# First attention's heads: column denominators, rows turned on TensorE, other step order

## What is computed

```python
w = jnp.exp(dmat - m_t[..., None]) * jnp.einsum('bhtd,bhsd->bhts', qc, kc)
num = jnp.einsum('bhts,bhsv->bhtv', w, vc) + wi[..., None] * jnp.einsum('bhvd,bhtd->bhtv', cm, qc)
den = jnp.sum(w, axis=-1) + wi * jnp.einsum('bhd,bhtd->bht', nv, qc)
h = num / jnp.maximum(jnp.abs(den), jnp.exp(-m_t))[..., None]
...
y = mlstm_readout(hl_f + rq(hl_b), ol, head_gain, w_out)   # norm of each head, gain, sigmoid(o), @ w_out
```

## Time and profile before

| | us |
|---|---|
| median of 3 runs | 1459.04 (1457.6 to 1459.34) |
| the profiled execution | 1456.49 |
| its span, first to last instruction | 1454.7 |
| PE busy | 1382.9 (95%) |
| DVE busy | 1146.6 (79%) |
| ACT busy | 784.0 (54%) |
| mean granted TensorE clock | 0.986 of 2.4 GHz |

### The profile page before, as it was taken

How to read it: one execution, slowest core, us unless ns; L and a number is a source line. 1 busy time by engine, 2 the same in 40 slices (tenths; PEclk the granted TensorE clock), 3 DMA queues, 4 the chain that set the end, 5 groups by cost and what they waited for, 6 DMA issues and landing times.

```text
span 1454.7 us, 19174 instructions
## 1 busy us (share of the span) xinstructions
PE 1382.9 (95%) x7530; PEld 1183.9 (81%) x7530; DVE 1146.6 (79%) x1629; ACT 784.0 (54%) x1114; POOL 1.4 (0%) x6
## 2 busy tenths in 40 slices
PE   6999988899998999999999999999999999999998
PEld 4888966788886888879887888878888888788886
DVE  5786688799977988878777988779889777887653
ACT  6613443666635555456356655376554555665542
POOL 0000000000000000000000000000000000000000
PEclk9999999999999999999999999999999999999999
DMA  9566413566793988866635877958878741585551
GB/s 384 214 244 249 147 49 130 219 254 234 258 340 138 327 289 293 319 233 229 251 129 187 306 277 287 335 192 302 286 287 304 269 154 60 202 280 198 187 189 58
DMA packets 62715, 337.79 MB, mean 232 GB/s; under 512 B 6929, under 2 KB 9361, under 8 KB 34209
## 3 DMA queue, kind: packets, MB, share of 16 engines
q1 hardware_dynamic: 62160, 335.35, 63.4%
q0 software_dynamic: 288, 1.05, 0.2%
q10 hardware_dynamic: 176, 0.16, 0.0%
HBM read 335.49 MB, written 1.05 MB: 231 GB/s over the span
## 4 chain that ended last, share of the span: by engine, by line
PE 80%; DVE 10%; ACT 5%; DMA 3%; issue 2%; SPq 0%; DVEq 0%; ACTq 0%
PE bank L253 77%; DVE wlo L249 2%; DMA raw<-w_stream 2%; ACT rstd L543 1%; ACT whi L242 1%; DVE mring L755 1%; ACT T L597 1%; DVE rd L1420 1%; PE bank L514 1%; DVE T L607 1%; DMA mring<-m_stream 1%; DVE SGC L672 1%; DVE X L685 1%; DVE EF L1422 0%; PE bank L730 0%
## 5 line engine op out<-in xcount | busy, mean ns | idle before, releaser
L253 PE MATMUL bank<-hh,whi 128*128 128x512 f32 (+1 forms) x2192 | 675.0, 368 | 8.3 <-DVE wlo L249 8.1
L249 DVE TENSOR_TENSOR wlo<-raw,whi 128x2048 fp32r<-128x2048 f32 x219 | 500.6, 2288 | 71.1 <-ACT whi L242 71.0
L253 PE MATMUL bank<-hh,wlo 128*128 128x256 f32 x1896 | 533.1, 281 | 0.0
L242 ACT ACTIVATE whi<-raw 128x2048 fp32r<-128x2048 f32 x219 | 418.4, 1915 | 163.6 <-PE bank L253 109.9
L253 PEld LDWEIGHTS bank<-hh,whi 128*128 128x128 f32 x2192 | 395.5, 190 | 85.0 <-DVE wlo L249 8.0
L253 PEld LDWEIGHTS bank<-hh,wlo 128*128 128x128 f32 x1896 | 360.5, 190 | 0.0
L253 PE MATMUL bank<-whi,hid_hi 128*128 128x512 f32 x440 | 172.2, 391 | 0.0
L253 PE MATMUL bank<-whi,hid_lo 128*128 128x512 f32 x440 | 171.3, 389 | 0.0
L253 PE MATMUL bank<-wlo,hid_hi 128*128 128x512 f32 x440 | 171.2, 389 | 0.0
L253 PE MATMUL bank<-whi,hh 128*128 128x512 f32 x480 | 158.4, 400 | 1.6 <-DVE hh L622 0.8
L755 DVE SCALAR_TENSOR_TENSOR mring<-mring,con 128x1024 f32<-128x1024 f32 x107 | 130.6, 1220 | 18.8 <-DMA mring<-m_stream 18.7
(11 more groups left out here) (293 smaller groups left out, 1305.2 us busy)
## 6 DMA issues: line engine op xcount, KB each, us to landing
raw<-w_stream SPq DMA_DIRECT2D x219, 1024.0 KB, 5.0
mring<-m_stream SPq DMA_DIRECT2D x139, 512.0 KB, 5.0
cb<-m_stream SPq DMA_DIRECT2D x53, 512.0 KB, 5.1
con<-const_d SPq DMA_DIRECT2D x1, 1472.0 KB, 11.4
XF<-xT SPq DMA_DIRECT2D x1, 1024.0 KB, 12.8
XC<-ctxT SPq DMA_DIRECT2D x1, 1024.0 KB, 12.8
y<-OUT SPq DMA_DIRECT2D x4, 256.0 KB, 2.6
cb<-c_row POOLq DMA_DIRECT2D x1, 512.0 KB, 7.7
```

The lines of the kernel that those rows point to most:

```text
L242: nc.scalar.activation(w_hi(c, 0, CW), raw[:, c % RAW_SLOTS], ACT.Copy).then_inc(s_hi, 1)
L249: nc.vector.tensor_tensor(w_lo(c, 0, CW), raw[:, c % RAW_SLOTS], w_hi(c, 0, CW).bitcast(f32), ALU.subtract).then_inc(s_lo, 1)
L253: return nc.tensor.matmul(out, lhsT, rhs, start=start, stop=True, skip_group_check=True)
```

## The change

Denominators are made as columns: `EF` is now the stationary operand and two columns of ones the moving one, so that the sums for 128 target tokens stand in 128 partitions of bank 3. ACT takes the absolute value of 128x4 numbers into `den`; DVE compares them with thresholds that were transposed once with `uc` (now 128x216), and inverts 128x4 numbers (`invert`). PE turns these columns into rows by four transposes of a broadcast column (`inverse_rows`) into the head's own bank, and `normalise` multiplies `EF` with that bank. `rows(h)` no longer broadcasts thresholds, `thb` is gone, the output gate moves to bank 5.

```diff
-        UP_UNITS = [[2, 1, 1, 0, 1] + [1, 0, 1, 1, 0] * 3 + [1, 0], [2, 1] + [1] * 20, [2, 1] + [1] * 20,
+        UP_UNITS = [[3, 2, 2, 1, 1] + [1, 0, 1, 1, 0] * 3 + [1, 0], [2, 1] + [1] * 20, [2, 1] + [1] * 20,
...
-                    mm(bank[2 + d][:, 0:SEQ], cst("sel")[0:36, q:q + P], mt[:], True)
-                    ins = mm(bank[2 + d][:, SEQ:], cst("sel")[0:36, q:q + P], th[:], True)
+                    ins = mm(bank[2][:, d * SEQ:(d + 1) * SEQ], cst("sel")[0:36, q:q + P], mt[:], True)
...
-                    for st in range(4):
-                        ins = mm(bank[5][:, d * SEQ:(d + 1) * SEQ], ones, EF[h % 2][:, d, st], st == 0)
+                    for t in range(2):
+                        at = 4 * t + 2 * d
+                        for st in range(4):
+                            ins = mm(bank[3][:, at:at + 2], EF[h % 2][:, d, st, t * P:(t + 1) * P], ones[:, 0:2],
+                                     st == 0)
                 ins.then_inc(s_den, 1)
 
-            def numerators(h):
-
-                pe.wait_ge(s_gw2, h + 1)
+            def inverse_rows(h):
+                pe.wait_ge(s_rc, h + 1)
                 if h >= 2:
                     pe.wait_ge(s_y, 2 * h - 2)
+                for d in range(2):
+                    for t in range(2):
+                        ins = nc.tensor.transpose(head_bank(h)[:, d * SEQ + t * P:d * SEQ + (t + 1) * P],
+                                                  den[:, h, t, d:d + 1].to_broadcast([P, P]), ident)
+                ins.then_inc(s_rb, 1)
...
+            for t in range(2):
+                ins = nc.tensor.transpose(bank[1][:, (4 + t) * 36:(5 + t) * 36], th[:, t * P:(t + 1) * P],
                                           ident[0:36, 0:36])
...
             denominators(0)
             scores(1)
+            inverse_rows(0)
+            rows(2)
             output_gate(2)
+            numerators(0)
             denominators(1)
             scores(2)
+            pe_stat(pe, N_LSTM)
+            inverse_rows(1)
             output_gate(3)
+            numerators(1)
+            rows(3)
+            denominators(2)
+            scores(3)
+            pe_stat(pe, N_LSTM + 1)
+            inverse_rows(2)
+            numerators(2)
+            denominators(3)
+            pe_stat(pe, N_LSTM + 2)
+            inverse_rows(3)
+            out_chunk(0)
+            numerators(3)
             pe.wait_ge(s_os, 4)
-            for h in range(HEADS):
-                if 1 <= h < HEADS - 1:
-                    denominators(h + 1)
-                if h == 1:
-                    scores(3)
-                if h >= 2:
-                    out_chunk(h - 2)
-                if h + 2 < HEADS:
-                    rows(h + 2)
-                numerators(h)
-                pe_stat(pe, N_LSTM + h)
-            pe.wait_ge(s_ad, HEADS)
             pe.wait_ge(s_y, 2 * HEADS - 2)
             pe_gate_row(pe, "lstm", (5, 6))
+            pe_stat(pe, N_LSTM + 3)
+            out_chunk(1)
             pe_out_last(pe, c + 15, 4, hhi, hlo, HEAD_TAIL, lambda: out_chunk(2), lambda: out_chunk(3))
...
+            def squares(h, table=False):
+                act_squares(act, N_LSTM + h, lambda j: head_bank(h)[:, j * SEQ:(j + 1) * SEQ],
+                            lambda j: (s_num, h + 1), table)
+
+            squares(0)
             magnitudes(1)
+            decay(2, 1)
+            decay(2, 0)
+            act_rstd(act, N_LSTM, DV)
             gate_read(3)
             act.wait_ge(s_os, 4)
             nc.scalar.activation(OS[:], OS[:], ACT.Sigmoid).then_inc(s_sg, 1)
-            for h in range(HEADS):
-                if 1 <= h < HEADS - 1:
-                    magnitudes(h + 1)
-                if h:
-                    round_head(h - 1)
-                    act_split(act, c + 14 + h)
-                if h + 2 < HEADS:
-                    decay(h + 2, 1)
-                act_squares(act, N_LSTM + h, lambda j: head_bank(h)[:, j * SEQ:(j + 1) * SEQ],
-                            lambda j: (s_num, h + 1), h == 0)
-                if h + 2 < HEADS:
-                    decay(h + 2, 0)
-                act_rstd(act, N_LSTM + h, DV)
-            act.wait_ge(s_arg, 4 * HEADS)
+            squares(1, True)
+            magnitudes(2)
+            decay(3, 1)
+            decay(3, 0)
+            act_rstd(act, N_LSTM + 1, DV)
+            round_head(0)
+            act_split(act, c + 15)
+            squares(2)
+            magnitudes(3)
+            act_rstd(act, N_LSTM + 2, DV)
+            round_head(1)
+            act_split(act, c + 16)
+            squares(3)
+            act_rstd(act, N_LSTM + 3, DV)
+            round_head(2)
+            act_split(act, c + 17)
...
-            mods(dve, 4)
...
-                mods(dve, 2)
+                mods(dve, 3)
...
+            def invert(h):
+
+                dve.wait_ge(s_ad, h + 1)
+                link(dve, nc.vector.tensor_tensor(den[:, h], den[:, h], uc[:, 4:6, h:36:32], ALU.max))
+                nc.vector.reciprocal(den[:, h], den[:, h]).then_inc(s_rc, 1)
+
             def normalise(h):
 
                 e = EF[h % 2]
-                dve.wait_ge(s_ad, h + 1)
-                link(dve, nc.vector.tensor_tensor(flat(rd[:]), flat(rd[:]), flat(thb[:, h]), ALU.max))
-                link(dve, nc.vector.reciprocal(flat(rd[:]), flat(rd[:])))
+                dve.wait_ge(s_rb, h + 1)
                 for d in range(2):
-                    ins = nc.vector.tensor_tensor(e[:, d], e[:, d], rd[:, d:d + 1].to_broadcast([P, 4, SEQ]),
-                                                  ALU.mult)
+                    row = head_bank(h)[:, d * SEQ:(d + 1) * SEQ].rearrange("p (a t) -> p a t", a=1)
+                    ins = nc.vector.tensor_tensor(e[:, d], e[:, d], row.to_broadcast([P, 4, SEQ]), ALU.mult)
...
-            mods(dve, 1)
+            mods(dve, 2)
             exponents(1)
             dve_split(dve, c + 12)
+            mods(dve, 2)
+            invert(0)
             weighted(1)
-            for h in range(HEADS):
-                normalise(h)
-                if h == 0:
-                    dve_split(dve, c + 13)
-                    dve_split(dve, c + 14)
-                else:
-                    finish_head(h - 1)
-                    if h > 1:
-                        dve_split(dve, c + 14 + h)
-                if h + 2 < HEADS:
-                    exponents(h + 2)
-                    if h == 1:
-                        dve_split(dve, c + 15)
-                    else:
-                        mods(dve, 2)
-                    weighted(h + 2)
-                elif h == 2:
-                    mods(dve, 2)
-            mods(dve, 1)
+            normalise(0)
+            dve_split(dve, c + 13)
+            exponents(2)
+            invert(1)
+            dve_split(dve, c + 14)
+            normalise(1)
+            weighted(2)
+            exponents(3)
+            finish_head(0)
+            invert(2)
+            normalise(2)
+            weighted(3)
+            dve_split(dve, c + 15)
+            finish_head(1)
+            invert(3)
+            normalise(3)
+            finish_head(2)
+            dve_split(dve, c + 16)
+            dve_split(dve, c + 17)
```

44 lines of the change are left out of this document (17 added, 27 removed).

## The result

The changed kernel takes 1470.21 us (median of 6 runs, 1467.51 to 1476.78) against 1458.87 us (median of 6, 1452.96 to 1459.93) for the kernel before: a ratio of 1.0094, 95% interval 1.0077 to 1.0111. It is slower by 11.3 us in the medians and by 14.0 us in the profiled executions (spans 1468.7 and 1454.7 us). The forecast was 4.5 us faster.

A forecast was written before the change was run, and what follows sets the result against it. PE was taken to bound the kernel, waiting in three places, with DVE late in the heads. Terms -6.0 - 1.5 - 4.9 + 0.6 + 7.3 = -4.5 us gave 1454.5 us from 1459.04, range 1448.5 to 1461.

The forecast's parts named there:

- the rest: Program from the first FFN's tile 5 to the end: no change forecast.
- Term 1: Near 77 us: moving four units from ahead of chunk 12's split removes PE's 3.25 us wait and 2.8 us lost clock; -6.0 us.
- Term 2: Rows of heads 0 and 1: no threshold broadcasts, 0.86 us less per head; -1.5 us.
- Term 3: Heads, first denominators to last output matmul: 94.9 us becomes 90.0 with column denominators; -4.9 us, bounds -10 and 0.
- the four long waits: PE's waits in the heads for DVE and ACT, placed at 2.7, 2.6, 3.6 and 2.6 us.
- rival (d): Heads: PE's clock sits at 1.2 GHz through most head steps; +8 us, 1462.8 us; dense output gates spoke against it; chance 0.07.
- Terms 4 and 5: Stage's end: DVE's boundary product later, +0.6 us; first FFN's head: moved units delay chunk 30's split, +7.3 us.
- The eighth unit: First FFN, right behind chunk 30's split: one more moved unit delays the next split by some 0.5 us.
- term 5: First FFN's head: seven units instead of four before chunk 30's split, rows landing late; +7.3 us, bounds 3.7 and 11.
- Rival (a): Heads give nothing, since waits around invert take more or the clock is low longer; +4.9 us, 1459.4 us; chance 0.17.

The follow-up runs named there:

- e3: Kernel before with only the early units moved as in the change (none ahead of the split of chunk 12); 1456.19 us, ratio 0.9994.
- e12: e3 plus the copies of V's second half moved forward on ACT and DVE; 1451.64 us, ratio 0.9960 to the kernel before.
- e1: Changed kernel with the denominators' moving operand 128 columns of ones wide instead of 2; 1460.98 us, ratio 1.0020 to the kernel before.
- e4: Kernel before with only the head loop's four units moved into the first FFN's head; 1461.43 us, ratio 1.0026.
- e11: e8 with the denominators 2 columns wide again; 1455.37 us, ratio 0.9992 to the kernel before.
- e2: Changed kernel with four units taken out of the first FFN's head and put back in the head steps; 1462.19 us, ratio 1.0024 to the kernel before.
- e6: Changed kernel with the copies of V's second half moved forward on ACT and DVE; 1468.42 us, ratio 1.0089 to the kernel before.
- e7: Changed kernel with the edits of both e1 and e2; 1450.99 us, ratio 0.9970 to the kernel before.
- e8: e7 with the last loop of finish_head(0) and (1) called later, behind normalise and weighted of the head two later; 1448.47 us, ratio 0.9946 to the kernel before.
- e10: e8 plus the copies of V's second half moved forward; 1446.70 us, ratio 0.9928 to the kernel before.
- e13: e10 with invert(0) moved ahead of the two units behind split c+12 on DVE; 1444.26 us, ratio 0.9911 to the kernel before.

## Why the prediction was wrong

The profiled executions missed the forecast by 14.0 + 4.5 = 18.5 us: 6.7 in terms 1 and 2, 14.3 in term 3, -0.2 in terms 4 and 5, and -2.3 in the rest.

**Term 1 (-6.0 us), half right, and lost downstream.** At its place it gave 5.9 us (scores(0) at 134.10 instead of 139.97) and the clock of 1.00. The step that failed is the one from the gap to what is late next: it looked at "the tightest place behind them", the read of the keys' banks, and stopped there. The read of V's second half further on had its copies behind decay(0) and two units, and DVE, held by rows that landed late (waits of 2.10 and 2.19 us; 1.31 and 1.33 before), came to exponents(0) at 134.75 us, 0.9 us later than before (133.89), while PE came 5.9 us earlier. The wait of 4.14 us and the low clock behind it took nearly all. Measured at the denominators, with term 2: -0.8 us; alone, e3, 0.9994; with V copied first, e12, 0.9960.

**Term 2 (-1.5 us), right.** From the first `mt` matmul to the denominators is 154.47 - 147.56 = 6.91 us in after, against 155.31 - 147.54 = 7.77 before: 0.86 us for one head as worked out. It comes in behind term 1's loss, so that the sum of both at the denominators is -0.8 and not -7.5.

**Term 3 (-4.9 us), wrong, +9.4 measured.** The placement of the steps held for the four long waits. The first short one, for `den` of head 0 (from 4.7 to 6.3), didn't come in after, where the scores behind the first set took 3.45 us instead of 1.8, and came in e1 with 1.39 us. What failed is the sentence on the clock: it let the clock fall only behind waits, 2.2 us in one place and 1.5 in the others, and never behind the narrow matmuls. PE spent about 42 us at 1.2 GHz. The mechanism was rival (d), priced at +8 against the forecast with a chance of 0.07; against it stood "the output gates are dense", but here a clock that fell during or behind the denominators stayed low over the scores and statistics (11.0 and 6.0 us in after, 5.7 and 4.1 in e1). Of the 104.3 - 90.0 = 14.3 us that the heads are over the forecast, e1 gives back 10.9; the other 3.4 are close to the denominators' own 3.7 us per head instead of 2.9, four times 0.8 = 3.2. For that price the Trainium skill ("TensorE: Matmul & The Clock Gate", section on LDWEIGHTS) had the better figure: columns / 1.2 ns makes 3.4 us for 32 pairs; the trace shows 3.67. The prediction set it aside for the loads of line 1043, which hold 4 partitions and stand in pairs with 16 matmuls of 4 columns. Those are 0.06 us apart, so the trace agrees with that figure for the loads with 128 partitions and not for these.

**Terms 4 and 5 (+0.6 and +7.3 us), right.** Together +7.7 us measured (44.9 against 37.2). The eighth unit's 0.5 us falls behind tile 5 and isn't in that, and terms 4 and 5 can't be told apart in one stretch. But term 5 was worked out for the FFN alone: e4 shows that the same four units had cost 5.0 us in the old heads, which the prediction held inside term 3 without a number of its own.

**The remainder.** -2.3 us in the rest of the two profiled executions is within the scatter of that stretch over all profiles.

**Readings and sums.** Rival (a) says that the heads before had fewer and shorter waits; the trace has eight from 177 us on, of 0.56 to 3.70 us and 12.5 us together, more than after's. Rival (d) says that the clock fell once in this stage before; the heads have three falls, 0.72 over 187 to 193 us, 0.72 over 205 to 211 us and 0.50 over 229 to 235 us. Both made the heads before look better kept than they were, and neither changes the sum. The steps that (d) adds to about 25 us come to 28 by the prediction's own durations. The range, at half of the way to the bounds of terms 3 and 5, would be 1450.2 to 1458.8, not 1448.5 to 1461.

The chance of slower, 0.08, rested on the case that came, and the range ended 9 us below the result. Rival (d) asked for 7.5 us more of lost clock; the trace of before held no two-column matmul from which to exclude it. Its narrowest are 16 of 4 columns (`L1043`), right behind a wait of 3.88 us, four transposes of 36 columns (`L1142`), and 48 of 64 columns from 727 to 744 us, in groups of six between wider ones, over which the clock stayed at 1.00. The sentence that named two-column matmuls as evidence for the rival should have been a bound of term 3: the heads' column-bound work outside the denominators, at half clock, is worth more than all that the change could win.

## What to carry to other kernels

Turning a reduction around so that it gives columns saves VectorE's time (a reciprocal of 3.35 us became 0.18 us here), but look at what TensorE streams meanwhile: 32 weight loads took 3.7 us with 2 columns and with 128, and the 2 column form lost the clock for the work behind it. Padding the moving operand to 128 columns, most of which nobody reads, cost nothing and gave back 7 to 11 us. The Trainium skill ("TensorE: Matmul & The Clock Gate", section "Why this matters for your kernels") advises, for thin matmuls that wait for DMA between bursts, to reorder the loop or pad them. Here the clock fell without such a wait; padding to 128 columns helped all the same (1.0020 against 1.0094), and padding to 32 did not (1.0089).

When a stall is removed, follow every engine's queue to the next places where they meet, not to the next tight place alone: here a copy queued behind an unrelated step took nearly all of the 6 us, and moving two calls gave 5 of them back in the kernel before.

Work moved away from the engine that sets the pace of one stage is free only if the stage that receives it has idle time; and once an engine waits for a neighbour (VectorE 7.7 us for ScalarE's rounding), call first the short step that a third engine is waiting for.

## What was not expected of the hardware

The granted clock fell to 1.2 GHz while TensorE was busy without a gap: 0.50 over 156 to 162 us in e11, whose last wait of PE ended at 139.76 us (2.81 us) and whose clock was 1.00 over 140 to 150 us. In the kernel before, every fall from 60 to 250 us stood behind waits: 3.25 us at 80.04, 2.58 and 0.84 us up to 188.19, 2.26 and 1.32 us up to 205.43, 3.70 us at 230.37. The same set of 32 matmuls took 3.5 us (154.47 to 158.01) and 5.2 us (197.08 to 202.30) within after, depending on where the clock fell.

How often and how long it falls differs between executions of nearly the same code: behind the second set the clock is 0.74 over 170 to 183 us in after and 0.87 in e2. The times don't scatter more for it: the 2 column kernels span 9 to 14 us (after 1467.5 to 1476.8, e6 1462.1 to 1476.5), the kernels with 128 columns 3 to 12 (e7 1446.9 to 1458.9), and the kernel before 14.7 in 35 runs (1450.9 to 1465.6).

Open stays why narrow matmuls lower the clock, from which width between 32 and 128 columns they don't, why the changed kernel with V copied first (e6) gains nothing in the median while its one profile is 4.6 us shorter than after's, and how much of e8's, e10's and e13's single steps is real, each being near what these runs can tell apart. Their sum is not in doubt.
